# Dots that read the normalised tokens from PSUM instead of SBUF

## The reference

```
q = (xt @ w_q).reshape(PEER_BLOCK, PEER_HEADS, 2, PEER_HALF)
...
act = jax.nn.gelu(jnp.einsum('thkd,td->thk', u_tab[idx], xt))
return jnp.einsum('thk,thkd->td', g * act, v_tab[idx])
```

## Time and profile before

| | |
|---|---|
| Median of 3 runs | 2186.98 us (2181.11 to 2188.45) |
| The profiled execution | 2193.73 us |
| Its span, first to last instruction | 2191.9 us |
| Granted TensorE clock, mean | 0.786 of full speed |
| Busy: PE, DVE, POOL, ACT | 71%, 64%, 55%, 16% |
| Moved by DMA | 751.57 MB, mean 343 GB/s |

### The profile page before, as it was taken

The page is one execution under the profiler, slowest core; times in us unless marked ns, Lnnn a source line. Parts: engine busy times, 40 slices in busy tenths (PEclk is TensorE's granted clock), DMA queues, the critical chain, the costliest instruction groups (busy, mean ns, idle before and its releaser), DMA issues. The chain is left out here.

```text
span 2191.9 us, 25755 instructions
## 1 busy us (share of the span) xinstructions
PE 1564.9 (71%) x9198; PEld 756.0 (34%) x9198; DVE 1394.2 (64%) x3469; ACT 356.0 (16%) x901; POOL 1202.2 (55%) x1097
## 2 busy tenths in 40 slices
PE   5676556876567779977797799877878770456566
PEld 2355223542133326443542355535424220112111
DVE  2447998597776655578689753687888327434541
ACT  0100112111112211113132110121312110011111
POOL 0004378544677465457566744564666457635675
PEclk8787768978768879988787798977968785577759
DMA  9719999999989799898899998987998989999998
GB/s 370 278 56 412 327 368 348 410 419 382 369 309 337 263 350 414 339 373 320 304 326 330 325 388 336 383 320 257 349 348 285 400 336 355 375 405 395 367 362 329
DMA packets 213942, 751.57 MB, mean 343 GB/s; under 512 B 27236, under 2 KB 35628, under 8 KB 213816
## 3 DMA queue, kind: packets, MB, share of 16 engines
q0 software_dynamic: 155136, 564.20, 68.8%
q1 hardware_dynamic: 58680, 185.72, 21.7%
HBM read 747.74 MB, written 2.10 MB: 342 GB/s over the span
## 5 line engine op out<-in xcount | busy, mean ns | idle before, releaser
L780 POOL DMA_INDIRECT uring<-in_peer_u,expert x512 | 585.7, 1144 | 498.3 <-DVE dots L1933 192.4
L1218 PE MATMUL yacc<-vring,diag 64*64 64x512 f32 x4096 | 662.4, 746 | 190.7 <-DMA vring<-in_peer_v,expert 126.6
L780 POOL DMA_INDIRECT vring<-in_peer_v,expert x512 | 542.0, 1059 | 434.9 <-PE yacc L1218 284.8
L1933 DVE CUSTOM_DVE_ANT_0 uring<-uring,h 128x1024 f32<-128x1024 f32 x512 | 613.7, 1225 | 164.5 <-DMA uring<-in_peer_u,expert 150.5
L1218 PEld LDWEIGHTS yacc<-vring,diag 64*64 64x64 f32 x4096 | 152.3, 156 | 580.4 <-DMA vring<-in_peer_v,expert 302.7
L1454 ACT ACTIVATE diag<-cst,wts 128x64 f32<-128x64 f32 (+1 forms) x528 | 173.0, 344 | 929.1 <-PE yacc L1218 694.0
L1006 PE MATMUL pp<-hT,wring 128*128 128x128 f32 x992 | 133.0, 296 | 18.3 <-issue 13.1
L1006 PEld LDWEIGHTS pp<-hT,wring 128*128 128x128 f32 x992 | 127.3, 210 | 30.8 <-issue 28.9
L1806 DVE TENSOR_REDUCE arena<-arena 128x16 f32<-128x1024 f32 x64 | 77.9, 1216 | 33.6 <-ACT arena L1393 24.6
L1069 PE MATMUL pp<-w_uk,arena 128*128 128x512 f32 x128 | 77.2, 693 | 14.4 <-issue 8.3
L1707 DVE MAX8 t<-sc 128x8 f32<-128x128 f32 (+1 forms) x68 | 19.9, 292 | 101.4 <-ACT sc L1254 60.8
(11 more groups left out here) (301 smaller groups left out, 1849.7 us busy)
## 6 DMA issues: line engine op xcount, KB each, us to landing
wring<-in_peer_w_q SPq DMA_DIRECT2D x47, 1024.0 KB
wring<-in_w_mod SPq DMA_DIRECT2D x38, 1024.0 KB
wring<-in_sg_w_in SPq DMA_DIRECT2D x48, 768.0 KB
wring<-in_sg_w_out SPq DMA_DIRECT2D x18, 1024.0 KB
wring<-in_mla_w_o SPq DMA_DIRECT2D x9, 1024.0 KB
uring<-in_peer_u,expert POOLq DMA_INDIRECT x512
vring<-in_peer_v,expert POOLq DMA_INDIRECT x512
uring<-in_w_mod SPq DMA_DIRECT2D x6, 1024.0 KB, 16.2
```

The source lines that it names most:

```text
L780: pool.indirect_dma_start(ring[:, slot % RING, :], None, table[n // 3], bass.IndirectOffsetOnAxis(ap=idx, axis=0)).then_inc(land[slot % RI ...
L1218: last = pe.matmul(yacc[64 * q:64 * q + 64, r], diag[at, slot % RING, :], v[at, 512 * q:512 * q + 512], start=first, stop=final)
L1933: dve.tensor_tensor_reduce(u, u, rows_h[:, :], 1.0, 0.0, ALU.mult, ALU.add, dots[:, p % 2, i:i + 1]).then_inc(u_used, 1)
```

## The change

Four things are done.
1. Ahead of the slots where (n, head) = (1, 2), (3, 0) and (4, 0) begin, DVE copies h_tok of the tile into the two banks of pq, and the dots from there on to the end of that tile read the tokens from pq. These are 96 + 128 + 128 = 352 of the 528 slots.
2. So that pq is free, its other users move: the cache stages keep the keys in the two banks of pp alone, one tile for each square (16 squares of 512 columns instead of 8 of 1024 in each of the 8 stages); the gated unit uses bank 0 of pp; the sample's value sums use bank 1 of ps; cache_init and the replicated sample tokens use pp and ps.
3. As bank 1 of ps then holds the sample's sums, peer_out for n >= 3 can't spread its gate into ps. Two stages "gate" do that ahead of time, one bank half at a time through ps[0], into gate_out, a part of the arena in SBUF.
4. The five lists of places are drawn anew for the changed stages.

```diff
+H_BANKS = {SLOT0[STEPS.index(s)]: s[0] for s in ((1, 2), (3, 0), (4, 0))}
+H_FROM = {n: g for g, n in H_BANKS.items()}
...
-    era2 = [("peer_out", 1)] + sgu(B) + woven(heads(4, (4, 4)), caches[CACHE0[2]:])
-    era3 = [("cache_out",), ("proj", S), ("norm", S, 0, 1), ("query_s", 2), ("topk_s", 2), ("peer_out", 3)]
+    era2 = [("peer_out", 1)] + sgu(B) + [("gate", 3)] + woven(heads(4, (4, 4)), caches[CACHE0[2]:])
+    era3 = [("cache_out",), ("proj", S), ("norm", S, 0, 1), ("query_s", 2), ("topk_s", 2), ("peer_out", 3), ("gate", 4)]
...
+        gate_out = wcT[:, 512:512 + D]
...
                     if second:
+                        after(pe, ACTE, k, "hT1")
                         for q in range(4):
                             at = slice(32 * q, 32 * q + 32)
-                            last = pe.matmul((pp, pq)[q // 2][:, q % 2, 0:QUAD], const("sel16")[at, :], h[at, :],
+                            last = pe.matmul((pp, pss)[q // 2][:, q % 2, 0:QUAD], const("sel16")[at, :], h[at, :],
...
-                def keys_of(j):
-                    if j >= 2:
-                        after(pe, ACTE, k, f"sq{j - 2}")
-                    for i in range(2):
-                        tile = 2 * j + i
-                        lhs = cTc[:, P * (tile % 8):P * (tile % 8) + P]
-                        pe.matmul(kn_bank[j % 2][:, i], lhs, w_uk[:, :], start=True, stop=True)
-                        last = pe.matmul(ps[0][:, H * tile:H * tile + H], lhs, qabs[:, b, :], start=False,
-                                         stop=True, skip_group_check=True)
-                    signal(last, f"kn{j}")
+                def keys_of(tile):
+                    if tile >= 2:
+                        after(pe, ACTE, k, f"sq{tile - 2}")
+                    lhs = cTc[:, P * (tile % 8):P * (tile % 8) + P]
+                    pe.matmul(pp[:, tile % 2], lhs, w_uk[:, :], start=True, stop=True)
+                    signal(pe.matmul(ps[0][:, H * tile:H * tile + H], lhs, qabs[:, b, :], start=False,
+                                     stop=True, skip_group_check=True), f"kn{tile}")
...
-                w, banks = chunk(k, 0, 1, SGH), (ps[0], ps[1], pq[:, 0])
+                w, banks = chunk(k, 0, 1, SGH), (ps[0], ps[1], pp[:, 0])
...
+            def gate(k, n):
+                begin(pe, k)
+                pe.wait_ge(mod_done[DVE], mod_count(mod_row(k)))
+                for i in range(2):
+                    if i:
+                        after(pe, DVE, k, "gate0")
+                    for q in range(2):
+                        one = 64 * i + 32 * q + NT
+                        last = pe.matmul(ps[0][:, 256 * q:256 * q + 256], ident[:, one:one + 1].to_broadcast([P, P]),
+                                         mrows[:, mod_row(k), :], start=True, stop=True)
+                    signal(last, f"row{i}")
...
-                spread(pss, mod_row(k))
+                if n < 3:
+                    spread(pss, mod_row(k))
...
+                elif first and h is None:
+                    after(pe, ACTE, WHERE[("query_s", n)], "s")
...
-                    last = quad_matmuls(pq[:, 1], diag[:, slot % RING, 0:32], v, QUAD, first, final)
+                    last = quad_matmuls(ps[1], diag[:, slot % RING, 0:32], v, QUAD, first, final)
...
-                    signal(act.activation(knsq[:, 1024 * (j % 2):1024 * (j % 2) + 1024],
-                                          kn_bank[j % 2][:, :, :].rearrange("p i n -> p (i n)"), ACT.Square), f"sq{j}")
+                    signal(act.activation(knsq[:, 512 * (tile % 4):512 * (tile % 4) + 512], pp[:, tile % 2], ACT.Square),
+                           f"sq{tile}")
...
-                    if SCHEDULE[k][0] == "peer_out":
+                    gates = gate_out if SCHEDULE[k][0] == "peer_out" and SCHEDULE[k][1] >= 3 else h
+                    if SCHEDULE[k][0] == "peer_out" and SCHEDULE[k][1] < 3:
                         link(cp(h, flat(pss)))
-                    link(tt(h, h, flat(acc), ALU.mult))
+                    link(tt(h, gates, flat(acc), ALU.mult))
...
+            def gate_early(k, n):
+                begin(dve, k)
+                for i in range(2):
+                    after(dve, PE, k, f"row{i}")
+                    signal(cp(gate_out[:, 512 * i:512 * i + 512], ps[0][:, :]), f"gate{i}")
...
+                if g in H_BANKS:
+                    dve.wait_ge(mod_done[DVE], len(MODS) // MOD_ROW)
+                    dve.wait_ge(u_used, g)
+                    chain(cp(flat(pq), rows_h[:, :]))
+                if n in H_FROM and g >= H_FROM[n]:
+                    rows_h = pq[:, :, :].rearrange("p q n -> p (q n)")
                 dve.wait_ge(u_land[g % RING], 16 * (g // RING + 1))
```

More of the change, by code:

```diff
@@ L335, in labels @@
         return ["row"] * (tile != S) + [f"w{i}" for i in range(6)], ["row"] * (tile != S) + ["x"], []
+    if kind == "gate":
+        return ["row0", "row1"], ["gate0", "gate1"], []
     if kind == "peer_out":
@@ L370 @@
 CHUNK_AT = {c: i for i, c in enumerate(CHUNKS)}
-PQ_USERS = ("attn", "cache_init", "cache")
+PQ_USERS = ("attn",)
 ARENA = 7680
@@ L388, in mod_row @@
         return 6 * s[2] + 3 * s[3]
-    if s[0] == "peer_out":
+    if s[0] in ("peer_out", "gate"):
         return 6 * (s[1] // 3) + 5
@@ L1086, in cache @@
                     after(pe, ACTE, k, f"cT{g}")
-                    if g == 0:
-                        tiles_T(1)
-                        keys_of(0)
-                        keys_of(1)
-                    else:
-                        if g < 3:
-                            tiles_T(g + 1)
-                        keys_of(2 * g)
-                        keys_of(2 * g + 1)
+                    if g < 3:
+                        tiles_T(g + 1)
+                    for i in range(4):
+                        keys_of(4 * g + i)
                     point(k, 1 + g)
@@ L1120, in sgu_init @@
                 for q in range(3):
-                    signal(transposes((ps[0], ps[1], pq[:, 0])[q], [sv[:, P * g:P * g + P] for g in range(4 * q, 4 * q + 4)], P),
+                    signal(transposes((ps[0], ps[1], pp[:, 0])[q], [sv[:, P * g:P * g + P] for g in range(4 * q, 4 * q + 4)], P),
                            f"wT{q}")
@@ L1230, in _ @@
                           sgu_init=sgu_init, sgu_v=sgu_v, sgu_u=sgu_u, sgu_mix=sgu_mix, sgu_s=sgu_s,
-                          sgu_s_mix=sgu_s_mix, sgu_out=sgu_out, peer_out=peer_out)
+                          sgu_s_mix=sgu_s_mix, sgu_out=sgu_out, gate=gate, peer_out=peer_out)
             for k, s in enumerate(SCHEDULE):
@@ L1273, in norm @@
                     for i in range(2):
-                        last = copy(h_rep[:, 512 * i:512 * i + 512].rearrange("p (q n) -> p q n", q=2), (pp, pq)[i][:, :, 0:QUAD])
+                        last = copy(h_rep[:, 512 * i:512 * i + 512].rearrange("p (q n) -> p q n", q=2), (pp, pss)[i][:, :, 0:QUAD])
                     signal(last, "rep")
@@ L1383, in latents, with squares @@
                     if g >= 2:
-                        after(act, PE, k, f"kn{2 * g - 3}")
+                        after(act, PE, k, f"kn{4 * g - 5}")
                     signal(copy(cTc[:, 512 * (g % 2):512 * (g % 2) + 512], ps[1][:, :]), f"cT{g}")
-                def squares(j):
-                    after(act, PE, k, f"kn{j}")
-                    if j < 2 and not rope_before(b):
+                def squares(tile):
+                    after(act, PE, k, f"kn{tile}")
+                    if tile < 4 and not rope_before(b):
                         after(act, DVE, k, "krsq")
-                    if j >= 2:
-                        after(act, DVE, k, f"ssn{j - 2}")
-                    signal(act.activation(knsq[:, 1024 * (j % 2):1024 * (j % 2) + 1024],
-                                          kn_bank[j % 2][:, :, :].rearrange("p i n -> p (i n)"), ACT.Square), f"sq{j}")
+                    if tile >= 4 and tile % 2 == 0:
+                        after(act, DVE, k, f"ssn{tile // 2 - 2}")
+                    signal(act.activation(knsq[:, 512 * (tile % 4):512 * (tile % 4) + 512], pp[:, tile % 2], ACT.Square),
+                           f"sq{tile}")
                 latents(0)
@@ L1399, in cache @@
                         latents(g + 1)
-                    squares(2 * g)
-                    squares(2 * g + 1)
+                    for i in range(4):
+                        squares(4 * g + i)
                     point(k, 1 + g)
@@ L1413, in sgu_v @@
                     for q in range(3):
-                        last = copy(sv[:, 512 * q:512 * q + 512], (ps[0], ps[1], pq[:, 0])[q][:, :])
+                        last = copy(sv[:, 512 * q:512 * q + 512], (ps[0], ps[1], pp[:, 0])[q][:, :])
                     signal(last, "v")
@@ L1963, in _ @@
                           sgu_vnorm=sgu_vnorm, sgu_mix=sgu_mix, sgu_s_mix=sgu_s_mix, sgu_out=sgu_out,
-                          peer_out=peer_out)
+                          gate=gate_early, peer_out=peer_out)
             for k, s in enumerate(SCHEDULE):
```

133 lines of the change are left out of this document (66 added, 67 removed).

## The result

The changed kernel takes 2238.24 us (median; 2231.09 to 2245.55), the kernel before beside it 2187.72 (2181.11 to 2189.59): a ratio of 1.0203 (95% interval 1.0161 to 1.0245), +50.5 us, where -24.2 was forecast. The predicted range was 2118 to 2203 us. Further down an interval stands in square brackets behind its ratio.

What follows compares the result with a forecast made beforehand. No engine was full; a ring of gathers, landings and dots or value sums bound it, POOL's gathers stretched by two-SBUF-input dots. -29.6 + 5.4 = -24.2 us on 2193.73 gave 2169.5, less 6.7 for the median: 2163 us, range 2118 to 2203.

Steps and rivals of the forecast that it cites:

- the lower bound of the relief: Gathers on POOL: least gain from shortening them set at nothing, landings being late next; the upper bound was all 106 us.
- Relief of the gathers: Gathers on POOL beside moved dots no longer stretched: 106 us of stretch removed, 29.6 us gained on the path.
- The dots themselves: DVE dots with one input in PSUM: 0 change each, bounds 0.02 us either way, 7 us over 352.
- Rival D: Gathers on POOL stay at 1.1 us beside PSUM dots, only costs are left: 2192 us, chance 0.06.
- Rival A: POOL is the bound far more than the chain of waits says, half of 106 us gained: 2139 us, chance 0.17.
- B: DMA bytes hide the relief, shorter gathers only queue behind a full DMA: about 2184 us, chance 0.14.
- Rival C: PE stopped in the cache stages waiting for squares, 60 us or more of waiting deciding it: 2209 us, chance 0.16.
- The two banks and stages together: Narrower cache stages and gate stages, within added costs of 10.7 us also covering copies and sample waits; half, 5.4, counted lost.
- The order: Redrawn places of dots, value sums, diagonals and gathers: 0 in the sum, 33 us either way in the range.
- What would show it: Signs of being right: gathers within 1 us, POOL near 1100 us, dots unchanged, rate near 420 GB/s, longer POOL waits.
- The fifth: Sign in the stretch where POOL is full: DMA rate near 420 GB/s, up from 366.
- The chances: Outcome odds for the whole kernel: faster 0.69, same 0.13, slower 0.18.

Runs made afterwards that it cites:

- e9: Small separate program, phases of value sums, dots, copies and gathers alone or together, gathers reading one row: 24 value sums 22.0, 22.9 us alone, 45.4, 41.4 beside gathers.
- e17: The changed kernel unaltered, timed again in a later sitting: 2053.63 us against 2078.83 for the kernel before, ratio 0.9865.
- e13: The kernel before with two memsets of 128 columns on POOL ahead of each gather from slot 160 on: 1.0702 to the kernel before.
- e11: The changed kernel with two memsets of 128 columns on POOL ahead of each gather from slot 160 on: 1.0355 to the kernel before.
- e2: The changed kernel with all dots reading the tokens from SBUF, copies into pq kept: 0.9986 to the kernel before.
- e4: The kernel before (four key banks, no gate stages, dots from SBUF) with the changed kernel's redrawn order: 0.9953 to the kernel before.
- e3: The changed kernel with dots from SBUF and the order of the kernel before, so only banks and gate stages differ: 1.006 to the kernel before.
- e10: Small separate program, value sums beside gathers of random rows, with varied spacing, short rows, plain loads or few outstanding: 24 value sums 20.2 to 23.2 us in every phase.

## Why the prediction was wrong

- **The failed step is the lower bound of the relief**, "Bounds: nothing (the landings are the next late thing...)", and with it all four rivals: I held that a shorter gather can help or be hidden, and not that it can harm. What the runs showed in its place: in the kind of sitting of the result, PE's signals come late where gathers follow each other every 1.24 us (e9: 41 to 45 us for 24 value sums that take 22 alone), in the kernel 163 us of lateness before and 250 after, and the 352 dots from PSUM cost 1.2 to 2.2 per cent where 29.6 us, 1.35 per cent, were counted as gained. The stretched gathers of the kernel before, up to 1.99 us beside a dot, would have held them apart; that part is argued. The row that should have warned stood in the kernel before: its waits "<- remote" on ACT, 170.7 us, on a program with one core. I read the chain and POOL's groups and not ACT's waits, as ACT was 16% busy.
- **Relief of the gathers**: as forecast in size. POOL 1107.3 us, the median 940 ns, the means in 736:2116 down by 183 and 79 ns; of 197 gathers beside dots from PSUM alone none is over 1 us. Where nothing is held up the whole sum came out, e17 with -25.2 us (-1.35% [-1.74, -0.96]) against -24.2. The closeness is luck in part: the sum was read from a trace of the first kind, with its late signals in the chain, and its terms weren't measured apart in the second. With slow gathers e13 and e11 give about half of the relief as time, where I had taken 28% of it from the chain.
- **The dots themselves**: 0 per dot, right (1.219 for 1.225; in e9 24 of them went 1.142 us apart from PSUM and 1.146 from SBUF). The Trainium skill ("Perfetto Trace Analysis", section "Optimizing Scalar/DVE Operations") has about 60 ns of overhead for DVE on SBUF and about 125 on PSUM; no such step shows here.
- **Rival D** fell: the relief is there. **Rival A** fell: POOL waits more, it isn't the bound; **B** fell: the rate sank to 334 GB/s from 348, where B would have kept it; in e17 it is 365 over the span, 342 before.
- **Rival C**, the slower side, had a similar time (2209) by another mechanism, and fell: L1073 waited 51.4 us for the squares, under the 60 named, by the list that gave 14.3 before (it adds the waits of its weight loads; by the page 23.1). That is 37 us more where I took 5; in e17, with the same two banks, the list has 15.0, under 1 more. So late signals lengthened it, as at 1542.39 above. The two banks and stages together cost 0.3 per cent (e2 against e4) to 0.6 (e3), 7 to 13 us for the 5.4 I counted.
- **The order**: 0 with 33 us either way; e4 shows -0.47% [-0.87, -0.07], 10 us, in the first kind. With two pads in the second kind it is 1.0732 for 1.0702: nothing gained.
- **What would show it**: four of the signs came out "right" (gathers, POOL's 1100, the dot, longer waits of POOL), beside a slower kernel. They tested the mechanism, and none of them tested whether it was the only one. The fifth would have told: 420 GB/s in the stretch where POOL is full. Its like here (1867:1938, again 50 gathers in 71 us) has 357, for 366 before; in e17 (1704:1775, 57 gathers) it has 404.
- The chances: 0.18 for slower was too little, since the bounds of one term were one-sided with a sign that nothing in the trace proved.

What stays open. What holds PE's signals up isn't shown. The trace itself is a suspect. The runs are taken with it, and a third of the semaphore updates is missing in just the sittings in which signals are late, more of them with all 352 dots from PSUM (16.8 to 17.6 thousand on record) than with none (18.2 to 18.5). So the 2 per cent may be a loss of recorded runs alone. The Trainium skill ("NOTIFIC — the notification-queue block", section "Overflow: three behaviours, one of which stalls the engine") says that inside the block records are held back rather than lost, and that a full queue, by its mode, drops records or stalls the producer; its section "Constraints, capacities, measured rates" has an implicit record cost the engine nothing. That would fit a stalled PE; no run here shows it. Nor was it found what makes a sitting one kind or the other, or whether gathers 1.6 us apart would heal the first kind: the runs made for it fell into the second. And e9 and e10 differ in their rows as well as in kind.

Neither version beats both in both kinds. In the first e4, the new order on the old banks, is best: 0.9953. In the second the changed kernel has 0.9865, and e4 wasn't timed there without the memsets.

## What to carry to other kernels

Before relieving an engine, look for waits in the trace of before that nothing recorded ends ("remote" on one core, "issue" in front of single matmuls): they are a sign of a second mechanism at work, and a change that packs transfers closer may feed it. Let no bound of a term end at zero because its mechanism can only help; the same instruction can pace something else. And where two results of one kernel differ by more than their intervals, compare what the kernel before does in each before explaining the change.

## What the hardware showed that I had not expected

- The same program of one core, the kernel before, ran in 2187.7 to 2221.5 us in five sittings and in 2078.8 to 2098.4 in three, 4 to 7% apart, and two chip numbers came up in both.
- In the first kind PE's completions come over 3 us late in 40 to 51% of cases where six or more gathers were issued in the 7 us before, and 24 value sums beside gathers take 41 to 45 us for 22, with no signal for up to 11.7 us (e9). In the second kind none of 3401 completions is. Whether the recording does it is open.
- A gather beside a dot with two SBUF inputs takes 1.45 us in the mean and up to 1.99 (e9; beside random rows 1.35 and 1.39 in e10), beside one with an input in PSUM 0.94.
- A memset of 128 columns on POOL, 0.22 us, mostly hides in the 0.30 us in front of a gather: it adds 0.09 us to the spacing.
